# A two-layer transformer kernel: the first sixteen modulation rows as column-tiled matmuls, an earlier eviction, and fused attention logits

## What is computed

```
c_act = silu(c)                                # 1024 numbers
mod = c_act @ w_ada + b_ada                    # 6 x 1024 numbers
shift1, scale1, gate1, shift2, scale2, gate2 = split(mod, 6)
h = rms_norm(x, norm1_g) * (1 + scale1) + shift1
proj = h @ w_in                                # q, k, v, low-rank gate input a_lr, r
log_a = log_sigmoid(a_lr @ w_gla_alpha + b_gla_alpha) / 16     # the decay
...
logits = q @ k.T + bias                        # dsa and nsa, per head
p = exp(logits - max(logits)) / sum(exp(logits - max(logits)))
```

## Time and profile before

| | |
|---|---|
| median of 3 runs | 1647.91 us (1647.88 to 1650.3) |
| the profiled execution | 1651.48 us |
| its span in the profile | 1649.7 us |
| granted TensorE clock, mean | 0.985 |
| instructions | 33146 |
| busy: TensorE, VectorE, ScalarE, GpSimd | 96%, 66%, 51%, 30% |
| moved by DMA | 288.72 MB, 175 GB/s |

### The profile page before, as it was taken

The page is one execution under the profiler, slowest core; times in us unless marked ns, Lnnn a source line. Parts: engine busy times, 40 slices in busy tenths (PEclk is TensorE's granted clock), DMA queues, the critical chain, the costliest instruction groups (busy, mean ns, idle before and its releaser), DMA issues.

```text
span 1649.7 us, 33146 instructions
## 1 busy us (share of the span) xinstructions
PE 1583.7 (96%) x10882; PEld 1438.6 (87%) x10882; DVE 1080.6 (66%) x2417; ACT 840.6 (51%) x1808; POOL 494.5 (30%) x489
## 2 busy tenths in 40 slices
PE   6999999999999999999999999789999999999998
PEld 4779899999999999887888878689999888889997
DVE  5676489648988895555555583856555654665555
ACT  3344455565555555554555552555454524655454
POOL 4111879887877773000000004210000101310000
PEclk9999899999999999999999999899999998999999
DMA  8862344444444444557555554137555642145554
GB/s 336 296 231 87 112 154 173 178 170 163 165 161 161 161 165 172 191 190 287 191 191 191 191 188 145 39 115 270 188 179 184 249 141 78 39 164 181 190 180 152
DMA packets 81474, 288.72 MB, mean 175 GB/s; under 512 B 10160, under 2 KB 11488, under 8 KB 81280
## 3 DMA queue, kind: packets, MB, share of 16 engines
q1 hardware_dynamic: 70144, 248.91, 42.8%
q0 software_dynamic: 9936, 35.79, 5.7%
q10 hardware_dynamic: 1328, 3.15, 0.5%
HBM read 285.19 MB, written 2.62 MB: 174 GB/s over the span
## 4 chain that ended last, share of the span: by engine, by line
PE 83%; DVE 6%; ACT 3%; issue 3%; POOL 3%; DMA 2%; DVEq 0%; ACTq 0%; POOLq 0%; SPq 0%
PE pu L657 13%; PE pu L658 13%; PE pu L659 13%; PE pacc L714 9%; PE pacc L716 8%; PE pacc L715 8%; PE pu L625 3%; PE pacc L1059 2%; PE pu L637 2%; PE pacc L657 2%; PE pacc L658 2%; PE pacc L659 2%; POOL ring_lo L436 2%; DMA ring<-in_weights 1%; DVE ring_lo L436 1%
## 5 line engine op out<-in xcount | busy, mean ns | idle before, releaser
L429 ACT ACTIVATE ring_hi<-ring 128x512 fp32r<-128x512 f32 x880 | 505.0, 622 | 374.6 <-PE pacc L716 195.0
L436 DVE TENSOR_TENSOR ring_lo<-ring,ring_hi 128x512 fp32r<-128x512 f32 x592 | 385.0, 692 | 338.0 <-ACT ring_hi L429 337.6
L657 PE MATMUL pu<-Xh,ring_hi 128*128 128x256 f32 x1472 | 426.1, 289 | 12.9 <-DVE Xl L1869 3.2
L658 PE MATMUL pu<-Xl,ring_hi 128*128 128x256 f32 x1472 | 419.1, 285 | 0.0
L659 PE MATMUL pu<-Xh,ring_lo 128*128 128x256 f32 x1472 | 418.6, 284 | 0.0
L436 POOL TENSOR_TENSOR ring_lo<-ring,ring_hi 128x512 fp32r<-128x512 f32 x288 | 370.8, 1310 | 92.5 <-ACT ring_hi L429 91.8
L657 PEld LDWEIGHTS pu<-Xh,ring_hi 128*128 128x128 f32 x1472 | 284.6, 193 | 21.8 <-issue 14.6
L658 PEld LDWEIGHTS pu<-Xl,ring_hi 128*128 128x128 f32 x1472 | 285.2, 194 | 0.2
L659 PEld LDWEIGHTS pu<-Xh,ring_lo 128*128 128x128 f32 x1472 | 285.0, 194 | 0.0
L714 PE MATMUL pacc<-ring_hi,vh 128*128 128x512 f32 x512 | 200.8, 392 | 3.8 <-DVE vl L2310 3.7
L716 PE MATMUL pacc<-ring_lo,vh 128*128 128x512 f32 x512 | 200.3, 391 | 0.0
(11 more groups left out here) (403 smaller groups left out, 2434.9 us busy)
## 6 DMA issues: line engine op xcount, KB each, us to landing
ring<-in_weights SPq DMA_DIRECT2D x472, 512.0 KB, 3.4
big<-in_ada POOLq DMA_DIRECT2D x40, 512.0 KB, 6.8
big<-in_w POOLq DMA_DIRECT2D x12, 512.0 KB, 7.4
bias_row<-big ACTq DMA_DIRECT2D x1, 1536.0 KB, 6.8
XT<-in_xT ACTq DMA_DIRECT2D x1, 1024.0 KB, 8.4
scr<-in_ada POOLq DMA_DIRECT2D x2, 512.0 KB, 12.4
tk<-in_ada POOLq DMA_DIRECT2D x2, 512.0 KB, 14.1
early_h<-in_ada POOLq DMA_DIRECT2D x2, 512.0 KB, 16.1
```

The lines of the kernel that those rows point to most:

```text
L429: nc.scalar.activation(ring_hi[:, n % 2, half], ring[:, n % RING, half], ACT.Copy).then_inc(s["split_hi"], 1)
L436: api.tensor_tensor(ring_lo[:, n % RING, half], ring[:, n % RING, half], ring_hi[:, n % 2, half], ALU.subtract).then_inc(s[LOW[name][0]], 1)
L657: mm(out, ring_hi[:, n % 2, w], xh, start=start, stop=False, skip_group_check=True)
L658: mm(out, ring_hi[:, n % 2, w], xl, start=False, stop=False, skip_group_check=True)
```

## The change

The 16 first rows of w_ada are stored the other way round, with 128 inputs on partitions and 1024 outputs along the row: for each input chunk c a row for scale1 and one for shift1. c comes as 8 columns within `cols` (32 bits each on 128 partitions) and goes through silu there (`c_cols`). In the loop that makes the relative-bias rows TensorE now also takes, per chunk c, four matmuls: the stationary operand is the column of c repeated 32 times, the moving one half of a row (512 outputs), and matmul b writes partitions 32b to 32b+31 of one PSUM bank (`mod_rows`), accumulating over c. VectorE copies the bank to SBUF, TensorE transposes four 128x128 pieces, VectorE picks the 16 columns and adds the bias in one instruction, and the scaling of `HTf` is divided: ScalarE takes the even chunks, VectorE the odd ones. The broadcast of c for the other rows is issued by ScalarE after the fourth relative-bias row, its silu follows the scaling. VectorE's six further modulation rows are moved from after the exponents to before L1963's wait. ScalarE evicts slot 0 right after the low-rank rows. SP's first two ring loads wait for 12 and 14.

In dsa and nsa the bias add and the maximum become one tensor_tensor_reduce that writes the negated logits and their minimum; the exponential is taken with scale -1.

Shortened: lines of context are left out; the table of columns gains the entry ("c", 8), and the last eight rows' waits count one silu more.

```diff
@@ -312,6 +312,7 @@
         iota_ps = paccf[:, 3 * 512:3 * 512 + P]
+        mod_rows, mod_turned = pu[:, 0, :], pu[:, 1, :]
         row_dram = nc.dram_tensor("bias_row", (NH, P, BROW), F32, kind="Internal").ap()
@@ -343,6 +344,7 @@
         early_l = sb("early_l", [P, 2 * D], F32, where["Xl"])[:, :]
+        mod_copy, c_cols = R[:, T:3 * T], gain[:, 0:C]
         first_rows = [aring[:, k, :] for k in range(ARING)]
@@ -352,7 +354,7 @@
-            return (n // 2, 2) if n < C else (2 + n // 4, 4)
+            return (n // 4, 4) if n < C else (n // 2 - 2, 2)
@@ -450,7 +452,7 @@
                 if k < 2:
-                    sp.wait_ge(s["ada_used"], 8 + 4 * k)
+                    sp.wait_ge(s["ada_used"], 12 + 2 * k)
                 sp.dma_start(ring[:, k, :], weights_d[k, :, :]).then_inc(slot_full[k], 16)
@@ -803,15 +805,31 @@
             pe.wait_ge(s["relb_spread"], 1)
-            for h in range(NH):
-                if h >= 2:
-                    pe.wait_ge(s["row_copied"], h - 1)
-                mm(row_bank(h)[:, 0:BROW], relb_all[0:NB, h, :], oneh[0:NB, :], start=True, stop=True)\
+            pe.wait_ge(s["c_silu"], 1)
+            for c in range(C):
+                if c >= 2:
+                    pe.wait_ge(s["row_copied"], c - 1)
+                mm(row_bank(c)[:, 0:BROW], relb_all[0:NB, c, :], oneh[0:NB, :], start=True, stop=True)\
                     .then_inc(s["row_psum"], 1)
+                group, rows = first_part(2 * c)
+                pe.wait_ge(ada_first[group], 16 * rows)
+                col = c_cols[:, c:c + 1]
+                for b in range(4):
+                    last = mm(mod_rows[b * 32:(b + 1) * 32, :],
+                              bass.AP(tensor=col.tensor, offset=col.offset, ap=[list(col.ap[0]), [0, 32]]),
+                              mod_row(2 * c + b // 2)[:, b % 2 * 512:(b % 2 + 1) * 512], start=(c == 0), stop=(c == C - 1),
+                              skip_group_check=True)
+                last.then_inc(s["row_psum"] if c == C - 1 else s["ada_used"], 1 if c == C - 1 else 2)
+            pe.wait_ge(s["relb_spread"], 2)
+            for q in range(4):
+                last = nc.tensor.transpose(mod_turned[:, q * P:(q + 1) * P], mod_copy[:, q * P:(q + 1) * P], ident[:, :])
+                if q == 0:
+                    last.then_inc(s["ada_used"], 2)
+            last.then_inc(s["row_psum"], 1)
...
             for c in range(C):
-                pe.wait_ge(s["h_chunks"], c + 1)
+                pe.wait_ge(s["h_chunks" if c % 2 == 0 else "h_scaled"], c // 2 + 1 + c % 2)
                 last = mm(pm[0:16, 0:T], walr[:, c, :], HTf[:, c, :], start=(c == 0), stop=(c == C - 1))
@@ -1432,10 +1450,11 @@
                     wid = keys_of(u) + (1 if kind == "swa" else 0)
-                    act.wait_ge(s["att_max"], u + 1)
+                    act.wait_ge(s["att_max" if kind == "swa" else "att_biased"], u + 1)
                     if u >= 4:
...
                     f(Px[:, u % 4, 0:wid], Sx[:, u % 4, 0:wid], ACT.Exp, bias=stats[:, u % 4:u % 4 + 1],
+                      scale=1.0 if kind == "swa" else -1.0,
                       accum_out=stats[:, 4 + u % 4:5 + u % 4]).then_inc(s["att_exp"], 1)
@@ -1472,11 +1491,10 @@
-            act.dma_start(cs, c_d.partition_broadcast(P)).then_inc(s["c_loaded"], 16)
             act.dma_start(XT[:, :, :], xT_d).then_inc(s["x_loaded"], 16)
             act.wait_ge(s["casts_made"], 1)
-            act.wait_ge(s["c_loaded"], 16)
-            f(cs, cs, ACT.Silu).then_inc(s["c_silu"], 1)
+            act.wait_ge(s["cols_loaded"], 16)
+            f(c_cols, cols[:, COL["c"]:COL["c"] + C], ACT.Silu).then_inc(s["c_silu"], 1)
             act.wait_ge(s["x_loaded"], 16)
@@ -1484,14 +1502,19 @@
                 f(brow[:, h, :], row_bank(h)[:, 0:BROW], ACT.Copy).then_inc(s["row_copied"], 1)
+                if h == 3:
+                    act.dma_start(cs, c_d.partition_broadcast(P)).then_inc(s["c_loaded"], 16)
             act.wait_ge(s["xn_ready"], 1)
-            for c in range(C):
-                act.wait_ge(s["h_scaled"], c + 1)
-                f(HTf[:, c, :], HTf[:, c, :], ACT.Identity, bias=mod[:, 2 * c + 1:2 * c + 2],
-                  scale=mod[:, 2 * c:2 * c + 1]).then_inc(s["h_chunks"], 1)
+            act.wait_ge(s["h_scaled"], 1)
+            for c in range(0, C, 2):
+                f(HTf[:, c, :], HTf[:, c, :], ACT.Identity, bias=mod[:, C + c:C + c + 1],
+                  scale=mod[:, c:c + 1]).then_inc(s["h_chunks"], 1)
+            act.wait_ge(s["c_loaded"], 16)
+            f(cs, cs, ACT.Silu).then_inc(s["c_silu"], 1)
...
             f(alr[0:16, :], pm[0:16, 0:T], ACT.Copy).then_inc(s["alr_copied"], 1)
+            evac(SLOT["w_in"], qs[:, 0, :], entry(USE["w_in"]), scale=float(SD) ** -0.5)
             act.wait_ge(s["z_psum"], 1)
@@ -1511,6 +1534,8 @@
                 n_slot = SLOT["w_in"] + i
+                if i == 0:
+                    continue
                 if i < 4:
@@ -1893,6 +1918,8 @@
                     bias(u, Sx[:, u % 4, 0:L], score_psum(u, banks)[:, 0:L])
+                    if kind != "swa":
+                        return
                     dve.wait_ge(s["att_biased"], u + 1)
@@ -1924,40 +1951,36 @@
                 for n in range(first, first + count):
-                    if n < 2 * C:
-                        k, rows = first_part(n)
-                        dve.wait_ge(ada_first[k], 16 * rows)
-                    else:
-                        dve.wait_ge(ada_full[n % ARING], 16 * ((n - 2 * C) // ARING + 1))
+                    dve.wait_ge(ada_full[n % ARING], 16 * ((n - 2 * C) // ARING + 1))
                     v.tensor_tensor_reduce(out=mod_row(n), in0=mod_row(n), in1=cs, scale=1.0, scalar=0.0,
...
             first = cols[:, COL["b_ada"]:COL["b_ada"] + 2 * C]
-            step(v.tensor_scalar(strided(first[:, 0:1], [[2, C]]), strided(first[:, 0:1], [[2, C]]), 1.0, None, ALU.add))
+            step(v.tensor_scalar(first[:, 0:C], first[:, 0:C], 1.0, None, ALU.add))
             dve.wait_ge(s["relb_loaded"], 16 * 2)
             v.tensor_copy(relb_all[0:NB, :, :], strided(relb[0:NB, 0:1], [[1, NH], [0, P]])).then_inc(s["relb_spread"], 1)
-            dve.wait_ge(s["c_silu"], 1)
-            modulation(0, 4)
             dve.wait_ge(s["roots"], NORM["n1"])
             v.reciprocal(R[:, 0:TT], R[:, 0:TT]).then_inc(s["inverses"], 1)
-            modulation(4, 2)
             dve.wait_ge(s["spreads"], 1)
...
             last.then_inc(s["xn_ready"], 1)
-            for c in range(3):
-                dve.wait_ge(s["ada_used"], 6)
-                v.tensor_tensor(mod[:, 2 * c:2 * c + 2], mod[:, 2 * c:2 * c + 2], first[:, 2 * c:2 * c + 2], ALU.add)\
+            dve.wait_ge(s["row_psum"], NH + 1)
+            v.tensor_copy(mod_copy, mod_rows).then_inc(s["relb_spread"], 1)
+            dve.wait_ge(s["row_psum"], NH + 2)
+            v.tensor_tensor(mod[:, 0:2 * C].rearrange("p (b q) -> p b q", q=4),
+                            strided(mod_turned[:, 0:1], [[32, 4], [P, 4]]), first.rearrange("p (b q) -> p b q", q=4), ALU.add)\
+                .then_inc(s["h_scaled"], 1)
+            dve.wait_ge(s["h_scaled"], 1)
+            for c in range(1, C, 2):
+                v.tensor_scalar(HTf[:, c, :], HTf[:, c, :], mod[:, c:c + 1], mod[:, C + c:C + c + 1], ALU.mult, ALU.add)\
                     .then_inc(s["h_scaled"], 1)
-            for c in range(3, C):
-                modulation(2 * c, 2)
-                dve.wait_ge(s["ada_used"], 2 * c + 2)
-                v.tensor_tensor(mod[:, 2 * c:2 * c + 2], mod[:, 2 * c:2 * c + 2], first[:, 2 * c:2 * c + 2], ALU.add)\
-                    .then_inc(s["h_scaled"], 1)
-            dve.wait_ge(s["h_chunks"], C)
+            dve.wait_ge(s["h_chunks"], C // 2)
             v.memset(stats[:, 0:1], 0.0).then_inc(s["normed"], 1)
...
+            dve.wait_ge(s["c_silu"], 2)
+            modulation(2 * C, 6)
@@ -1980,7 +2003,6 @@
             v.tensor_scalar(kp, kp, 80.0 * GATE_TEMP, None, ALU.min).then_inc(s["ex_ready"], 1)
-            modulation(2 * C, 6)
@@ -2429,11 +2451,15 @@
+            def negative_logits(u, S, ps, added):
+
+                v.tensor_tensor_reduce(out=S, in0=ps, in1=added, scale=-1.0, scalar=3.0e38, op0=ALU.add, op1=ALU.min,
+                                       accum_out=stats[:, u % 4:u % 4 + 1]).then_inc(s["att_biased"], 1)
+
...
                 tt, h = UNITS[u][1:3]
-                L = keys_of(u)
                 dve.wait_ge(s["att_prebias"], u - SPAN["dsa"][0] + 1)
-                v.tensor_tensor(S, ps, S, ALU.add).then_inc(s["att_biased"], 1)
+                negative_logits(u, S, ps, S)
@@ -2577,7 +2603,7 @@
                 L = keys_of(u)
-                v.tensor_tensor(S, ps, Bt[:, UNITS[u][2], T - L:T], ALU.add).then_inc(s["att_biased"], 1)
+                negative_logits(u, S, ps, Bt[:, UNITS[u][2], T - L:T])
@@ -2666,14 +2692,16 @@
-    by_chunk = [i for c in range(C) for i in (C + c, c)] + list(range(2 * C, MOD))
```

(15 more changed lines are left out.)

## The result

The changed kernel takes **1655.49 us** (median of 10 runs, 1652.65 to 1662.73) against 1649.76 us (10 runs, 1647.88 to 1651.13) of the kernel before, run beside it on the same chip: ratio 1.0046, 95% interval 1.0035 to 1.0057, so it is slower. The ratio is that of the means (1656.94 and 1649.44 us, 7.5 apart); the medians are 5.7 us apart. The forecast was 1655.0, 7.2 above the median that was known then. The profiled execution took 1655.13 us with a span of 1653.4; that of before had 1651.48 and 1649.7, so between the two traces the difference is 3.7 us. That is 2 us less than between the medians, since the profiled execution of before lay above its own median by 1.7 us.

A forecast was written before the change was run, and what follows sets the result against it. TensorE was taken to bound the kernel (busy 96% of the span, 83% of the chain). Front +15.2, eviction -4.0 and logits -4 gave +7.2 us, 1655.0 us in the median's terms; range 1640 to 1662, the forecast's own 1651 to 1660.

The forecast's parts named there:

- front: Stretch up to the first projection, from x's transfer through the loop and low-rank matmuls: +15.2 us without the eviction.
- (a): At the front, sixteen reductions leave VectorE, 1.14 us each in the chain, 18 us together.
- (b): At the front, c's broadcast leaves the queue ahead of x, so x gains 1.4 us (0 to 2.8).
- (c): Tiled modulation matmuls in the loop: a chunk's four overlap, 0.94 us at 2.4 GHz, 1.87 at 1.2.
- (d): Bias rows between chunks: loop stays at 1.2 GHz, 3.3 us a chunk including 0.15 for turning, 26.4 us in all.
- (e): After the loop: a tail of 2.8 us, then low-rank matmuls of 5.5 us (3.4 to 6.9), ending at 53.8.
- (f): Slot 0 evicted ahead of the decay: TensorE's wait and the clock's fall behind it go, -4.0 us (-2.7 to -4.0).
- (g): Six reductions moved ahead of the decay on VectorE, late c and SP's later slot loads: all cost nothing.
- Late logits: Two late attentions: VectorE's separate maximum pass goes, -2 us in each (0 to -4).
- Rival A: Clock rises during the front loop, no record-length limit from 32-row matmuls; loop ends at 34.4, total 1641.5 us; chance 0.25.
- Rival B: Smaller costs: no switching cost, x earlier still, low-rank matmuls fast from the middle, attention -6; about +2, 1650 us; chance 0.15.
- Rival C: The attention gives nothing, TensorE and ScalarE being as slow there: +11.2, 1659 us; chance 0.15.

The follow-up runs named there:

- x4_full_height: Changed kernel with the relative-bias matmuls' operands zero-padded from 32 to all 128 rows; 1641.86 us, ratio 0.9959 to the kernel before.
- x5_rows_first: Changed kernel with all eight 32-row bias matmuls ahead of the chunks instead of one before each; 1647.96 us, ratio 0.9994 to the kernel before.
- x1_evict: Kernel before with only the eviction of slot 0 moved ahead of the decay; 1645.88 us against 1648.59, ratio 0.9982.
- x6_tiled_alone: Kernel before with the tiled modulation rows alone, old eviction place and two-pass logits; 1665.6 us against 1649.29, ratio 1.0094.
- x2_fused: Kernel before with only the fused logits in the two late attentions; 1644.74 us against 1648.59, ratio 0.9977.
- x3_evict_fused: Changed kernel with its first sixteen modulation rows back on VectorE, so eviction and fused logits alone; 1641.33 us, ratio 0.9954 to the kernel before.
- x8_padded_no_tiles: x3_evict_fused with the bias rows zero-padded to all 128 rows, no column tiles; 1642.71 us, ratio 0.9965 to the kernel before.

## Why the prediction was right

The forecast named the mechanism (the loop stays at 1.2 GHz, because 32-row matmuls stand between the tiled ones) and the sign. It said +7.2 us; measured were +5.7 between medians and +7.5 between means. That 1655.0 lies within 0.5 us of the median is partly luck: the median of before moved from 1647.91 (3 runs) to 1649.76 (10 runs), which made up for the difference. In the terms of the profiled execution the forecast was 1658.7, against 1655.13 measured. The parts, forecast and read from traces: front +15.2 and +16.6, eviction -4.0 and -4.6, logits -4 and -5.3, together +7.2 and +6.7. The other 3 us are the sum of the places where only one of the two executions had a low clock, above all the 1.9 us in the second attention of before. Point by point:

(a), (b) **x earlier.** L812 started at 18.21, 2.3 us before L809's 20.5, where I took 1.4 with 2.8 as the bound. The step that "the small silu and its table load end before x is there" was wrong: x's transfer was issued at 0.93 and landed 5.6 us later, at 6.5, while before it landed at 9.7. But the transfer of `cols` landed only at 5.9, and behind it ScalarE loaded its table and did the small silu until 7.47. That path, not x, started the front.

(c) **The tiled matmuls** took 1.87 us a chunk at the slow level, as worked out from L1294, and 0.99 at the fast one in x4_full_height, against 0.94. The slow number is right with some luck: it holds a turn of the array. In x5_rows_first, where tiled matmuls follow one another, each set of four records starts 0.853 us after the last at the low level and 0.43 at the high one, so a chunk alone is 1.71 or 0.86 us, and the 1.87 us between the starts in the earlier trace rows hold one turn, too.

(d) **The bias rows and the turning.** A chunk took 3.44 us, not 3.3: the two turns cost 3.44 less 1.28 less 1.71, so 0.45 us, where the forecast had the 0.16 inside its 1.87 and the allowance of 0.15. At the fast level with full-height rows they cost 1.83 less 0.64 less 0.86, so 0.33. "TensorEngine Tiling (Array Packing)", Key Properties, in the Trainium skill has the drain at a change of mode without a price; here it is a third to a half of a microsecond a chunk. The loop took 27.6 us instead of 26.4.

(e) **The tail** took 3.0 us (45.77 to 48.77), forecast 2.8. **L833** took 6.42, forecast 5.5 with 6.9 as the bound: by the two prices in the forecast, about 14 of its 16 records were slow (14 x 0.43 + 2 x 0.21 = 6.4). The clock rose 5.7 us after its start, at 54.5, not 4.2. Front: +16.6 instead of +15.2, from -0.9, +1.2, +0.2 and +0.9.

(f) **The eviction** took 4.6 us out of the trace (+16.6 to +11.9), forecast 4.0; in the medians of x1_evict it is worth 2.7, the other end of the range, with an interval that holds both. The clock's fall behind the wait was taken as certain from one execution; x6_tiled_alone had the wait without it.

(g) **The moved work** cost nothing, and the cover is read off: the last of the six reductions ended at 61.9, the decay's input on VectorE came at 65.88, and VectorE waited 3.98 us for it. Four microseconds of cover are left. No wait of TensorE stands behind the second projection.

**Late logits.** Forecast -4 in all, -2 in each attention. The median of x2_fused says -3.9, the lengths of the attentions in the traces -2.7 and -2.6. The price of the fused operation per column and its read was right.

**Rival A** fell by its own sign: no record of L812 below 842 ns. But its sum was good. Made to happen in x4_full_height, the case "the clock rises in the first chunk" gave a loop end at 33.7 (worked out 34.4), the end of the low-rank matmuls at 39.85 (40.2), and 1641.86 us (1641.5). What decided between 1641 and 1655 was the clock. The sentence of "TensorE: Matmul & The Clock Gate", Part 1, in the Trainium skill, that sustained matmul activity releases the throttle, is true here for full-height operands and not for 32-row ones: 16 such records back to back for 10.5 us in x5_rows_first, and a loop with them in every chunk for 27.6 us, released nothing. **Rival B** was right in two terms, the earlier start (0.9 us more than forecast) and the logits (-5.3, it had -6), and wrong in the other two: the turning and L833 came out dearer, not cheaper. **Rival C** is excluded by x2_fused. The three theories besides the forecast are gone too, with the one reservation made at x5_rows_first: the tiled form isn't slow (0.99 us a chunk), the turning costs 0.45 us of 3.44 and, between full-height shapes, doesn't hold the clock, and x3_evict_fused and x6_tiled_alone put the loss wholly into the modulation.

One thing stays open. The changed kernel's ten runs spread over 10 us, those of before over 3; its slowest two, 1661.41 and 1662.73 us, have a mean granted clock of 0.984 and its fastest, 1652.65, has 0.989. Where in the span those executions lose clock isn't known, since the profiled one is near the median.

## What to carry to other kernels

Before work is moved from a slower engine to TensorE, read from durations, not from the printed clock, at which level TensorE works at that place, and price the moved work at that level; here the same change was worth -7 us (x4_full_height) or +6 (between medians), by the clock almost alone. If small-height matmuls stand in such a stretch, pad their operands with zeros to the full height: it costs a few memsets on an engine that waits and no columns on TensorE, and lets the matmuls after them run at the high level. And a gain from an early finish ahead of a wait can be lost behind it, as in x8_padded_no_tiles, where the clock fell with the longer pauses. Last, before the gain of one part is read from two traces, look whether a kernel that leaves this part alone shows the same difference; x1_evict did here, by 1.9 us.

## What was unexpected of the hardware

- Height counts for the clock, and busy time doesn't suffice: with 32 rows in use, 842 ns for 384 columns for as long as the stretch lasted (27.6 us of a loop); with 96 rows of zeros added, 847 ns at first and 486 soon after, in x4_full_height and in x8_padded_no_tiles. The added rows are all zeros, and the clock rose all the same.
- Four fp32 matmuls on four column tiles overlap: 8 records of 512 columns take 0.99 us together at the high level with the turning, 0.86 without it, and 592 ns is the shortest single one.
- Turning the array costs 0.33 us per pair of turns between 128x128 matmuls and column tiles at the high level, and 0.45 between 32x128 ones and column tiles at the low level.
- After the same wait of 2.72 us the clock fell in two executions (48 records in 12.29 and 12.28 us) and stayed up in a third (10.60 us).
- The printed granted clock was 1.00 from 20 to 30 us, where every record of TensorE had the duration of 1.2 GHz. The first record of the clock in the trace stands at 54.5 us (at 36.4 in the kernel before, at 20.2 in x4_full_height), in each case where the durations fall; ahead of it the table prints 1.00 without a record.
